# Hymba encoder layer on one core: quarter sums for the norms, loads made a stage ahead, and an addition moved to GpSimd

## What is computed

```
n = rms_norm(x);  proj = n @ w_in                      # r, k, v, q_diff, k_diff, v_diff
rkv = centred_conv(proj[..., :1536])                   # three taps along the tokens
delta = 0.5 * (prev(n) + next(n)) - n
g = sigmoid((n + delta * mix_g) @ gate_g1) @ gate_g2   # 1024 -> 160 -> 512
w_d, a_d = low-rank products of n + delta * mix_w[d], n + delta * mix_a[d]   # 1024 -> 64 each, d = 0, 1
y = RWKV-7 scan in both directions (8 heads x 64)
q, k = partial_rope(rms_norm(q_diff)), partial_rope(rms_norm(k_diff))   # 4 heads x 2 x 64, norm over each 64
lam = exp(sum(l0*l1)) - exp(sum(l2*l3)) + 0.2
att = (softmax(q1 k1) - lam * softmax(q2 k2)) @ v_diff
x += concat(group_norm(y) ..., rms_norm(att)) @ w_out;  x += swiglu(rms_norm(x))
```

## Time and profile before

| | us |
|---|---|
| median of 3 runs | 2425.66 (2424.18 to 2429.47) |
| profiled execution | 2425.8 |
| its span | 2424.0 |
| TensorE / VectorE / ScalarE / GpSimd busy | 2185.1 / 1109.1 / 829.0 / 349.6 |
| low-rank stage `lora_in` | from 385.4 |
| `prep` | from 481.6 |
| `solve_and_attention_in` | from 640.9 |
| `attention` | from 774.4 |

### The profile page before, as it was taken

One profiled execution on the slowest core, in us unless ns is written; L12 is line 12 of the kernel. 1 busy time (PEld: TensorE's weight loads), 2 busy tenths in 40 slices (PEclk: granted clock), 3 DMA queues, 4 the chain that ended last, 5 costly groups with the idle time before them and its releaser, 6 DMA issues. The chain is left out here.

```text
span 2424.0 us, 41479 instructions
## 1 busy us (share of the span) xinstructions
PE 2185.1 (90%) x17078; PEld 1848.6 (76%) x17078; DVE 1109.1 (46%) x1561; ACT 829.0 (34%) x1354; POOL 349.6 (14%) x360
## 2 busy tenths in 40 slices
PE   6999998867497888867999799999999999999999
PEld 5888884344397555556887489999998899999987
DVE  5432106679665766683777643232332232332221
ACT  6111114666474444444444322222222122222211
POOL 0000000000002999054454200000000000000000
PEclk8999999966667899977999899999999999999999
DMA  3222222045784000136884534222223332222232
GB/s 124 80 97 81 93 76 88 21 175 206 258 246 152 1 1 1 53 97 142 190 191 114 181 123 165 87 74 78 69 94 106 122 114 77 73 74 78 78 118 69
DMA packets 133762, 258.47 MB, mean 107 GB/s; under 512 B 11040, under 2 KB 81056, under 8 KB 132224
## 3 DMA queue, kind: packets, MB, share of 16 engines
q1 hardware_dynamic: 133632, 256.63, 33.3%
HBM read 184.69 MB, written 68.93 MB: 105 GB/s over the span
## 5 line engine op out<-in xcount | busy, mean ns | idle before, releaser
L215 PE MATMUL ff_acc<-normed_nh,normed_ff_low 128*128 128x320 f32 x1344 | 416.6, 310 | 6.3 <-SPq L163 5.2
L217 PE MATMUL ff_acc<-normed_nh,normed_ff_high 128*128 128x320 f32 x1344 | 416.3, 310 | 0.0
L216 PE MATMUL ff_acc<-normed_nl,normed_ff_high 128*128 128x320 f32 x1344 | 416.2, 310 | 0.0
L2727 DVE TENSOR_TENSOR normed_ff_low<-normed_ff_raw,normed_ff_high 128x1024 fp32r<-128x1024 f32 x126 | 154.4, 1226 | 427.7 <-ACT normed_ff_high L2691 427.5
L215 PEld LDWEIGHTS ff_acc<-normed_nh,normed_ff_low 128*128 128x128 f32 x1344 | 253.2, 188 | 7.0 <-SPq L163 5.4
L216 PEld LDWEIGHTS ff_acc<-normed_nl,normed_ff_high 128*128 128x128 f32 x1344 | 253.2, 188 | 0.0
L217 PEld LDWEIGHTS ff_acc<-normed_nh,normed_ff_high 128*128 128x128 f32 x1344 | 253.1, 188 | 0.0
L2691 ACT CAST normed_ff_high<-normed_ff_raw 128x1024 fp32r<-128x1024 f32 x126 | 131.8, 1046 | 234.6 <-PE ff_acc L217 233.8
L216 PE MATMUL ff_acc<-normed_ff_low,ff_hh 128*128 128x512 f32 x420 | 163.4, 389 | 0.0
L215 PE MATMUL ff_acc<-normed_ff_high,ff_hl 128*128 128x512 f32 x420 | 163.4, 389 | 0.0
L217 PE MATMUL ff_acc<-normed_ff_high,ff_hh 128*128 128x512 f32 x420 | 163.4, 389 | 0.0
(11 more groups left out here) (330 smaller groups left out, 4269.7 us busy)
## 6 DMA issues: line engine op xcount, KB each, us to landing
ch_ops<-dram_sx SPq DMA_DIRECT2D x88, 256.0 KB, 5.7
normed_ff_raw<-in_w_gate SPq DMA_DIRECT2D x44, 512.0 KB, 3.2
normed_ff_raw<-in_w_up SPq DMA_DIRECT2D x44, 512.0 KB, 3.3
normed_ff_raw<-in_w_down SPq DMA_DIRECT2D x44, 512.0 KB, 3.6
dram_sx<-pr_sx SPq DMA_DIRECT2D x7, 2816.0 KB, 8.1
pj_packed<-in_w_in SPq DMA_DIRECT2D x24, 512.0 KB, 4.6
heads_vt<-dram_sx SPq DMA_DIRECT2D x44, 256.0 KB, 4.7
dram_proj<-pj_mixed SPq DMA_DIRECT2D x12, 656.0 KB, 3.3
```

Of the source, the lines that this page charges most:

```text
L215: nc.tensor.matmul(out, ll, rh, start=start, stop=False)
L216: nc.tensor.matmul(out, lh, rl, start=False, stop=False)
L217: return nc.tensor.matmul(out, lh, rh, start=False, stop=stop)
L2727: nc.vector.tensor_tensor(low[s][:, :], raw[s], high[s][:, :].bitcast(F32), ALU.subtract).then_inc(cut_low[s], 1)
```

## The change

In `lora_in`, `gate_rows` sends each item once, for rows 0 to 127. After every fourth item, `gate_quarters` sends the four last items to four 32-row quarters of `acc2` with the weights of rows 128 to 159, so each quarter holds a partial sum over a fourth of the features. ScalarE copies the four quarters (`keep_partial`), and a product with a fixed matrix `fold` adds them, after the second round of direction 0. The late sigmoids follow.

At the start of `prep` nine more loads are issued: the first raw rows, cosines, sines, four small matrices, and the first two v blocks, into tiles on the right side of the SBUF that live through the next stage.

In `solve_and_attention_in` the squares are summed by four products, each with the [128, 32] matrix `quarter_mean` and a quarter of the tokens (328 columns), into a 32-partition quarter of `psq`: partitions 32q and 32q + 1 hold the two halves' means for the tokens of quarter q. `inverse` and `root` then work on 328 columns, and the spread is a product of six pieces with `quarter_heads`. The first two v blocks are turned at the start; blocks 2 and 3 are loaded in turns 0 and 1. GpSimd adds the sine and cosine parts. At the end ScalarE copies head 2, from other banks.

In `attention` the lambdas are made after the first unit's largest values, and the first scores wait for no constants.

```diff
# shape_constants
+    out["quarter_mean"] = np.zeros((P, BLK), np.float32)
+    out["quarter_mean"][:, 0:2] = out["head_mean"]
+    out["quarter_heads"] = np.zeros((P, P // BLK * P), np.float32)
+    for q in range(P // BLK):
+        out["quarter_heads"][BLK * q:BLK * q + 2, q * P:(q + 1) * P] = out["head_sum"].T
+    out["fold"] = (row[:, None] % BLK == np.arange(BLK)[None, :]).astype(np.float32)
...
# lora_in, SP
+                sp.dma_start(fold[:, :], g.small_of("fold")).then_inc(fold_in, 16)
...
+                sp.wait_ge(fold_kept, 1)
                 sp.dma_start(g.hidg_dram[0:GL - P, 1, :], hidg[0:GL - P, 1, :]).then_inc(stored, 16)
# lora_in, TensorE
                 def gate_rows(k):
                     pe.wait_ge(mixed_s, k + 1)
                     for n in range(TN):
-                        wd = CUTS[n + 1] - CUTS[n]
-                        for out, lo, rows in ((acc, 0, P), (acc2, P, GL - P)):
-                            last = nc.tensor.matmul(out[n][0:rows, 0:wd], wg[:, k * GL + lo:k * GL + lo + rows],
-                                                    mixed[k % SLOTS][:, CUTS[n]:CUTS[n + 1]], start=k == 0, stop=k == KT - 1)
-                    last.then_inc(used, 1)
+                        nc.tensor.matmul(acc[n][:, 0:CUTS[n + 1] - CUTS[n]], wg[:, k * GL:k * GL + P],
+                                         mixed[k % SLOTS][:, CUTS[n]:CUTS[n + 1]], start=k == 0, stop=k == KT - 1)
+                def gate_quarters(k0):
+                    for n in range(TN):
+                        for q, rows in enumerate(QUADS):
+                            lo = (k0 + q) * GL + P
+                            last = nc.tensor.matmul(acc2[n][rows, 0:CUTS[n + 1] - CUTS[n]], wg[:, lo:lo + BLK],
+                                                    mixed[(k0 + q) % SLOTS][:, CUTS[n]:CUTS[n + 1]], start=k0 == 0, stop=k0 == KT - 4)
+                            if n == TN - 1:
+                                last.then_inc(used, 1)
+                def fold_quarters():
+                    pe.wait_ge(fold_in, 16)
+                    pe.wait_ge(partial_kept, 1)
+                    for n in range(TN):
+                        last = nc.tensor.matmul(acc2[n][0:BLK, 0:CUTS[n + 1] - CUTS[n]], fold[:, :], partial[:, CUTS[n]:CUTS[n + 1]],
+                                                start=True, stop=True)
+                    last.then_inc(folded, 1)
...
                 for k in range(KT):
                     both_rows(0, k, acc)
+                    if k == 1:
+                        fold_quarters()
+                pe.wait_ge(fold_kept, 1)
# lora_in, ScalarE
-                keep(0, [(hidg[:, 0, :], acc, slice(0, P), ACT.Sigmoid), (hidg[:, 1, :], acc2, slice(0, GL - P), ACT.Sigmoid)])
-                for j in range(ENDS[0] + SLOTS, ENDS[1] + SLOTS):
+                keep(0, [(hidg[:, 0, :], acc, slice(0, P), ACT.Sigmoid)])
+                keep_partial()
+                for j in range(ENDS[0] + SLOTS, ENDS[0] + SLOTS + 4):
+                    weigh(j)
+                act.wait_ge(folded, 1)
+                keep(0, [(hidg[:, 1, :], acc2, slice(0, GL - P), ACT.Sigmoid)], fold_kept)
+                for j in range(ENDS[0] + SLOTS + 4, ENDS[1] + SLOTS):
# prep, SP (after load_v(1))
+                for to, of in ((g.raw_first, g.proj[3 * FT * P:(3 * FT + 1) * P, :]), (g.cos_sb, g.cos), (g.sin_sb, g.sin),
+                               *((t, g.small_of(name)) for name, t in g.ahead_small.items())):
+                    sp.dma_start(to[:, :], of).then_inc(ahead_in, 16)
+                for rows_at in range(2):
+                    _lo, _hi, at, n = RANGES[rows_at]
+                    sp.dma_start(g.v_rows[rows_at][:, :, 0:n], g.proj[2 * RW:3 * RW, at:at + n].rearrange("(f p) t -> p f t", p=P)
+                                 ).then_inc(ahead_in, 16)
# solve_and_attention_in, SP
-                    if t == 1:
-                        sp.wait_ge(v_zeroed, 2)
-                        load_v(0)
-                        load_v(1)
+                    if t < 2:
+                        load_v(t + 2)
+                        store_v(t)
# GpSimd
+                for t in range(TILES):
+                    pool.wait_ge(sined, t + 1)
+                    pool.wait_ge(cosed, t + 1)
+                    nc.gpsimd.tensor_tensor(rot[t % 2][:, :], nrm[:, :], rot[t % 2][:, :], ALU.add).then_inc(added, 1)
# TensorE
-                    token_sums(nc, psq, sq[t % 2], heads[:, :]).then_inc(sums, 1)
+                    for q, quad in enumerate(QUADS):
+                        last = nc.tensor.matmul(psq[quad, 0:QTOK], mean[:, :], sq[t % 2][:, q * QTOK:(q + 1) * QTOK], start=True, stop=True)
+                    last.then_inc(sums, 1)
...
-                    spread(nc, psn, rows[t % 2], ident, TOK).then_inc(spreads, 1)
+                    for lo, hi in zip(BANK_CUTS, BANK_CUTS[1:]):
+                        q = lo // QTOK
+                        last = nc.tensor.matmul(psn[:, lo:hi], heads[:, q * P:(q + 1) * P], rows[t % 2][:, lo - q * QTOK:hi - q * QTOK],
+                                                start=True, stop=True)
+                    last.then_inc(spreads, 1)
...
-                pe.wait_ge(padded, 2)
+                pe.wait_ge(g.v_zeroed, 2)
+                turn_v(0)
                 sum_up(0)
+                turn_v(1)
+                pe.wait_ge(v_copied, 2)
                 part(0)
...
-                turn_v(0)
+                turn_v(2)
                 pe.wait_ge(roped, TILES)
                 turn_heads(0)
-                for j in range(1, HEADS):
-                    turn_v(j)
-                    turn_heads(j)
+                turn_v(3)
+                for h in range(1, HEADS):
+                    turn_heads(h)
# ScalarE
-                    nc.scalar.activation(rows[t % 2][:, :].rearrange("p (a b) -> p a b", b=HD), by_rows(st[t % 2][:, 1, :], 2),
-                                         ACT.Sqrt).then_inc(rooted, 1)
+                    nc.scalar.activation(rows[t % 2][:, :], st[t % 2][:, :], ACT.Sqrt).then_inc(rooted, 1)
...
                 square(0)
+                act.wait_ge(g.sx_stored[0], g.sx_stores[0])
+                keep_v(0)
+                keep_v(1)
+                root(0)
                 square(1)
-                root(0)
                 keep(0)
...
+                for h in ACT_HEADS:
+                    keep_heads(nc.scalar.copy, act, h).then_inc(heads_by_act, 1)
# VectorE
-                    nc.vector.tensor_scalar(st[t % 2][:, 0, :], psq[:, 0:2 * TT], 1e-6, None, ALU.add).then_inc(meaned, 1)
+                    nc.vector.tensor_scalar(st[t % 2][:, :], psq[:, 0:QTOK], 1e-6, None, ALU.add).then_inc(meaned, 1)
                     dve.wait_ge(meaned, t + 1)
-                    nc.vector.reciprocal(st[t % 2][:, 1, :], st[t % 2][:, 0, :]).then_inc(inverted, 1)
+                    nc.vector.reciprocal(st[t % 2][:, :], st[t % 2][:, :]).then_inc(inverted, 1)
...
-                    dve.wait_ge(sined, t + 1)
-                    dve.wait_ge(cosed, t + 1)
-                    nc.vector.tensor_tensor(rot[t % 2][:, :], nrm[:, :], rot[t % 2][:, :], ALU.add).then_inc(added, 1)
# attention, TensorE
-                pe.wait_ge(consts, PRIMED + 32)
...
-                for k in range(ALL + 1):
+                score(0)
+                pe.wait_ge(ident_in, PRIMED + 16)
+                for k in range(1, ALL + 1):
# attention, VectorE: the lambdas' eight instructions, before the loop until now
+                    if k == 0:
+                        lambdas()
```

More of the change, by code:

```diff
@@ L142, in ps, with far @@
         return self.enter_context(self.nc.psum_tensor(f"{self.stage}_{name}", list(shape), F32))
+    def far(self, name, shape):
+        return self.enter_context(self.nc.sbuf_tensor(f"{self.stage}_{name}", list(shape), F32, side="right"))
     def sem(self, name):
@@ L471, in lora_in @@
         hidg = c.sb("hidg", (P, 2, PTOK))
+        partial, fold = c.sb("partial", (P, TOK)), c.sb("fold", (P, BLK))
+        assert GL - P == BLK
         acc = [c.ps(f"acc{n}") for n in range(TN)]
@@ L588, in weigh, with keep @@
                                          ).then_inc(weighted, 1)
-                def keep(turn, parts):
+                def keep(turn, parts, kept=copied):
                     act.wait_ge(used, ENDS[turn])
@@ L598, in keep, with keep_partial @@
                                     last = nc.scalar.activation(dst[rows, p + x0 - a:p + x1 - a], ps[n][rows, x0 - lo:x1 - lo], func)
-                    last.then_inc(copied, 1)
+                    last.then_inc(kept, 1)
+                def keep_partial():
+                    for n in range(TN):
+                        last = nc.scalar.copy(partial[:, CUTS[n]:CUTS[n + 1]], acc2[n][:, 0:CUTS[n + 1] - CUTS[n]])
+                    last.then_inc(partial_kept, 1)
                 act.wait_ge(factors, 2)
@@ L700, in _ @@
                     last.then_inc(zeroed, 1)
+                for rows_at in range(2):
```

(18 more changed lines are left out.)

129 lines of the change are left out of this document (67 added, 62 removed).

## The result

The changed kernel took 2405.06 us (median; 2399.38 to 2413.28) where the kernel before, on the same chip, took 2427.56: ratio 0.9922, 95% interval 0.9904 to 0.9941. By the ratio that is 19 us, about 0.8%, faster; 2391 was forecast, and 2405.06 lies 1 us above the range. A second series gave 2407.14 and 0.9927 (0.9903 to 0.9951).

A forecast was written before the change was run, and what follows sets the result against it. TensorE was seen busy without a gap in the gate's products and the preparation's loop, whose beginning hangs on transfers. Savings 15 + 5.4 + 7.6 + 5.5 + 1.6 = 35.1 from 2425.8 gave 2391 us; range 2380 to 2404, from its bounds 2380 to 2400.

The forecast's parts named there:

- Quarters in the gate: Low-rank stage: four 32-row quarter products work at once, a set taking 2.2 us; 15 us saved, bounds 10 and 17.
- Added loads at nothing: RWKV preparation: nine more DMAs issued by SP, some 3.3 MB, cost nothing; 11 us if their cover were gone.
- Beginning 5.4: Start of the attention's preparation: tile 1's product with the norms at 675 instead of 680.45; 5.4 us saved, bounds 3 and 8.
- End 5.5: End of the attention's preparation: last blocks and heads take 14.6 us instead of 20.1; 5.5 saved, bounds 3.5 and 6.
- Attention's start 1.6: Attention: the first difference starts right behind the lambdas, at 780.75 instead of 782.39; 1.6 us saved.
- Loop 7.6: Loop of the attention's preparation: six turns shrink from 12.07 to 10.8 us each; 7.6 us saved.
- The turn of 10.8: Attention's preparation loop: length taken for one turn, 10.8 us instead of 12.07, chosen between TensorE's rings at both clocks.
- rings of 6.5 and 11.5 us: Attention's preparation loop: TensorE's work per turn (spread, three parts, sums), 6.5 us at 2.4 GHz, 11.5 at 1.2 GHz.
- ScalarE has 8.80 of 12 us and loses 0.9: Attention's preparation loop: ScalarE is busy 8.80 of 12 us and its work shrinks by 0.9.
- Nothing in the change reaches past the attention: Second half of the span: said to be untouched by the change, so no saving or loss was forecast there.
- GpSimd as the bound: Rival, attention's preparation: GpSimd's addition takes 5.3 us, ring 12.6, loop and beginning give nothing; 2404 us, chance 0.13.
- DMA in the loop: Rival, attention's preparation: DMA bounds the loop, half of the loop's and beginning's gain lost; 2397 us, chance 0.12.

The follow-up runs named there:

- experiment 4: The low-rank part alone (`lora_in` and its fold matrix) put into the kernel before: 2408.74 us, ratio 0.9944.
- experiments 3 and 6: 3: changed kernel with `below` stored ahead of the turn's loads, 2398.16 us, 0.9905; 6: that with the addition back on VectorE, 2396.18, 0.9878, again 2402.03, 0.9894.
- the same kernel in two groups: Changed kernel with `below` stored ahead of the turn's loads and the addition on VectorE, run twice: 2396.18 us (0.9878) and 2402.03 us (0.9894).
- 28 products: Changed kernel with early `below` store and addition on VectorE, plus 28 unused 32x32 products starting the stage that writes out attention and solves: 2391.47 us, 0.9861.

## Why the prediction was wrong, step by step

- **Quarters in the gate: right.** Four at once, 2.41 us a set; stage 14.5 us shorter for 15. The Trainium skill ("TensorE: Matmul & The Clock Gate", "Measured speedup vs the span model") has three column tiles at 2.38 times one; the prediction's estimate by it made a set 0.6 us longer than 2.2. Here four took 2.41 us where one pass took 2.39: four at the price of one.
- **Added loads at nothing: right** within the scatter of that stage, by experiment 4. **Beginning 5.4:** 4.9. **End 5.5:** 5.4. **Attention's start 1.6:** 1.6.
- **Loop 7.6: the step that failed.** Its prices were good (reciprocal, addition, sums 0.76 or 1.32 us, root 0.46), one was not: the spread, put at 2.45 or 4.40, took 4.0 to 5.0 in 12 instructions as it took 3.7 to 4.9 in 22. The turn of 10.8 came out all the same, once the store was early (65.4 / 6 = 10.9); that is in part luck, since 10.8 was picked between rings of 6.5 and 11.5 us that held the spread at too low a price. What failed is "ScalarE has 8.80 of 12 us and loses 0.9": busy time says nothing of what an engine waits for in order. Its copies stand behind a store which SP issues after the turn's loads, and the root that the next turn needs stands behind the copies. The wait was in the trace of before, 7.0 us, harmless under a TensorE that was busy in 71.70 of 73 us. I had asked which work hides each edit, but not which waits the busy TensorE was hiding. Cost: 6 us.
- **"Nothing in the change reaches past the attention": the second failed step**, 6 to 8 us, nearly as much. Five traces in which the attention's preparation is the new one, and no product is added, have the stage at 67.9 to 70.6 us; four with the old preparation at 60.2 to 64.7, and at equal clocks the gap stays (0.56: 67.9 and 68.0 against 62.8). The change takes 192 products and their loads from TensorE's stream and adds 6 products and their loads: 372 fewer instructions, which is one portion of 254 and 118 more. The stalls moved by 113, from 400 to 513. In the low-rank part alone, 12 more instructions moved them by 14, from 400 to 386, and nothing was lost.
- **The rivals.** GpSimd as the bound, and DMA in the loop: neither bounds it (experiments 3 and 6), though their 2404 and 2397 lie nearer to 2405 than the forecast does: the right size by another cause. The addition of 5.3 us, the first rival's price, took 2.97.
- **The range.** The bounds of the five terms add up to 21.1 and 44.0 us saved, 2382 to 2405; "2380 to 2400, from the bounds" is narrower at its slow end without a reason. Neither has a term for the stage behind the attention.

**What stays open.** Why a portion that begins at a set's first instructions costs more than one that begins in its middle is argued, not shown: in the middle, the code for the next set may come while TensorE waits at the set's start for ScalarE's copy; at the start, the wait for the copy and that for the code add up. That code is what TensorE waits for is inferred from the spacing, the packets' size, the 2.4 to 2.9 us from a packet's start to the end of a stall, and the effect of the count. The rest of the attention (2.5 us saved) and the stages behind (1.8 lost) lie in the scatter: the same kernel in two groups had medians of 2396.2 and 2402.0. So of the 8 to 11 us between the medians with and without 28 products, the stage's 3.1 are explained and the rest is not; the intervals of the two ratios overlap.

## What to carry to other kernels

When a change relieves an engine that was hardly ever idle, list every wait of the other engines in that stretch before costing it, however short and harmless: here one of 7.0 us came back as 10.9 to 11.3 and cost 6. Where TensorE runs sets of more than a hundred tiny products between waits, as here, its code seems to be a resource too, and a change elsewhere can shift where its portions begin; compare unchanged stages between the traces first, and test with a few idle products before blaming the clock. A part that buys nothing once the others are in (here the addition on GpSimd) is found only by undoing it alone.

## What the runs showed of the hardware that was not expected

- Code came in packets of 16384 bytes. TensorE's unwaited stalls in sets of tiny products were 254 instructions apart, up to 5.02 us long beside the stage's loads, 0.4 to 1.5 us later, and the early ones ended 2.4 to 2.9 us after a packet's start. Moving them by 112 instructions changed a 68.0 us stage to 64.9; moving them in the kernel before by 140 changed 60.2 to 64.7 into 69.4.
- One 32x32 product in 32-bit floats makes four instructions: 28 of them took the stage from 1448 products and as many loads to 1504 of each.
- The spread got no cheaper by fewer instructions and columns: at the lower clock 12 instructions for 1312 columns took 5.04 us, 22 for 1408 columns took 4.90.
- Four products with 32 output rows each, on four quarters of the array, took 2.41 us for 1312 columns each, one alone 2.39.
